# Order of the first stage, and of the last head pair, in an RWKV-7 and dilated-attention trunk

## What is computed

```python
h = rms_norm(x, mix_norm[0])
xx = jnp.pad(h, ((0, 0), (1, 0), (0, 0)))[:, :-1] - h      # token difference
x_mix = h[None] + xx[None] * mu[:, None, None, :]          # six mixes
rkv = jnp.einsum('cbsd,cde->cbse', x_mix[:3], w_rkv)       # receptance, key, value
w, a, g use x_mix[3], x_mix[4], x_mix[5] through low-rank products
...
outs, lses = per group: rms-normed q, k; banded softmax; o = probs v
weights = jax.nn.softmax(jnp.stack(lses), axis=0)
o = jnp.sum(weights[..., None] * jnp.stack(outs), axis=0) @ w_o
x = x + y; x = x + swiglu_ffn(rms_norm(x, ffn_norm[layer]), ...)
```

## Time and profile before

| | us |
|---|---|
| median of 3 runs | 1839.15 |
| profiled execution | 1842.12 |
| its span | 1840.3 |
| TensorE busy | 1799.3 |
| VectorE busy | 877.2 |
| ScalarE busy | 758.8 |

### The profile page before, as it was taken

How to read it: one execution, slowest core, us unless ns; L and a number is a source line. 1 busy time by engine, 2 the same in 40 slices (tenths; PEclk the granted TensorE clock), 3 DMA queues, 4 the chain that set the end, 5 groups by cost and what they waited for, 6 DMA issues and landing times.

```text
span 1840.3 us, 36149 instructions
## 1 busy us (share of the span) xinstructions
PE 1799.3 (98%) x15618; PEld 1371.4 (75%) x15618; DVE 877.2 (48%) x1513; ACT 758.8 (41%) x1292; POOL 196.8 (11%) x172
## 2 busy tenths in 40 slices
PE   8999999989999999999999999999999999999999
PEld 3746666656468888888888788788787788888887
DVE  6724444444264444433454654554555544444322
ACT  4434444432243223222456666666656542232211
POOL 0033333332100000000111111111010000000000
PEclk9999999989999999999999999999999999999999
DMA  3311222130123332323222222222222132323332
GB/s 113 118 64 51 75 68 67 63 120 29 36 80 103 94 101 92 103 92 103 93 80 92 81 65 86 81 71 79 81 75 86 51 99 93 103 92 96 100 102 92
DMA packets 57541, 155.00 MB, mean 84 GB/s; under 512 B 5591, under 2 KB 22535, under 8 KB 57384
## 3 DMA queue, kind: packets, MB, share of 16 engines
q1 hardware_dynamic: 57288, 152.63, 25.6%
q10 hardware_dynamic: 96, 0.07, 0.0%
HBM read 150.51 MB, written 11.61 MB: 88 GB/s over the span
## 4 chain that ended last, share of the span: by engine, by line
PE 69%; ACT 3%; DVE 1%; issue 1%; ACTq 0%
PE bank L548 67%; PE bank L551 2%; ACT f L1578 2%; DVE f L2094 0%; ACT f L1565 0%; ACT f L1591 0%; ACT r L1556 0%; ACT f L1552 0%; ACT f L1583 0%; ACT r L1268 0%; DVE r L1966 0%; DVE r L1682 0%; DVE f L2087 0%; ACT L1532 0%; ACT f L1279 0%
## 5 line engine op out<-in xcount | busy, mean ns | idle before, releaser
L548 PE MATMUL bank<-r 128*128 128x512 f32 x5424 | 1256.5, 391 | 1.9 <-DVE f L1999 0.7
L548 PEld LDWEIGHTS bank<-r 128*128 128x128 f32 x5424 | 1012.2, 188 | 225.1 <-issue 12.3
L548 PE MATMUL bank<-f 64*64 64x64 f32 (+5 forms) x9762 | 511.3, 257 | 30.5 <-issue 6.2
L548 PEld LDWEIGHTS bank<-f 64*64 64x64 f32 (+3 forms) x9762 | 311.2, 141 | 218.3 <-issue 126.4
L1682 DVE TENSOR_TENSOR r<-f,r 128x1024 fp32r<-128x1024 f32 x222 | 274.8, 1238 | 397.2 <-ACT r L1268 397.2
L1268 ACT ACTIVATE r<-f 128x1024 fp32r<-128x1024 f32 x222 | 232.5, 1048 | 147.7 <-PE bank L548 141.5
L2286 POOL TENSOR_TENSOR r<-f,r 128x512 fp32r<-128x512 f32 x48 | 62.1, 1295 | 845.0 <-ACT r L1556 845.0
L1535 ACT ACTIVATE r<-f 128x512 fp32r<-128x512 f32 x44 | 27.8, 632 | 215.6 <-DVE f L2005 215.6
L2035 DVE TENSOR_TENSOR f<-bank,f 128x512 f32<-128x512 f32 x72 | 56.2, 780 | 73.4 <-PE bank L548 70.1
L1532 ACT ACTIVATE f<-f 128x512 f32<-128x512 f32 x44 | 27.8, 632 | 110.5 <-DVE f L1995 110.5
L1565 ACT ACTIVATE f<-bank,f 128x512 f32<-128x512 f32 x48 | 32.9, 686 | 94.9 <-PE bank L548 94.9
(11 more groups left out here) (106 smaller groups left out, 911.9 us busy)
## 6 DMA issues: line engine op xcount, KB each, us to landing
f<-stream SPq DMA_DIRECT2D x245, 512.0 KB, 3.4
bias_copies<-bias_rows SPq DMA_DIRECT2D x6, 1536.0 KB
f<-xT SPq DMA_DIRECT2D x16, 256.0 KB, 4.5
f<-lora_out SPq DMA_DIRECT2D x16, 128.0 KB, 6.2
f<-bias_copies SPq DMA_DIRECT2D x16, 128.0 KB, 3.1
f<-bias_copies SPq DMA_DIRECT2D x32, 64.0 KB, 3.0
outT<-f SPq DMA_DIRECT2D x8, 256.0 KB, 4.4
f<-wo_last SPq DMA_DIRECT2D x2, 512.0 KB, 7.4
```

Of the source, the lines that this page charges most:

```text
L548: return nc.tensor.matmul(out, lhsT, rhs, start=start, stop=stop, skip_group_check=True)
```

## The change

In the first stage:
- ScalarE makes (1 - mu) h also for the value mixes (into `O_MIXV`) and the receptance mixes (into the temporaries), and VectorE adds mu h' in place. Value mixes no longer need the token differences.
- The token differences are made in pairs, ahead of each pair of decay and gate mixes, beside tiles 3 to 6.
- Both key tiles are multiplied chunk by chunk in turn, in banks 0 and 1; the value tile goes to bank 5.
- The value weights go to a place of their own (`O_VIN`), and the raw slots are counted accordingly.
- ScalarE's transfers of the bias rows come after the rounding of all receptance mixes and the split of panel `PAN_R + 1`.

In the last head pair: the three functions `last_pair` go. The general loop runs once more (`it` = 8) with the projection parts left out, and a table `EARLY` puts 14 chunks of output tiles 0 and 1 at four places. The other 50 chunks follow behind the combination of the last pair. Output tiles use two banks again, `ASIDE` goes, and weights before the feed-forward are split one panel later (`(n == 2)`).

```diff
-            if T_WO1 <= t < T_IN1:
-                return banks[(t - T_WO1) % 4]
...
-        ASIDE = {split_of(PAN_WO1 + 3): (O_XG + 4 * S, O_XG + 14 * S), split_of(PAN_WO1 + 4): (O_XG + 12 * S, O_QR)}
...
-                held = p - RAW - (RAW if p - RAW == PAN_WA else 0)
+                held = p - RAW - (RAW if p - RAW in (PAN_V, PAN_WA) else 0)
+                if p == PAN_V:
+                    sp.dma_start(f(O_VIN, 1024), stream[p]).then_inc(s["w_v"], 16)
+                    return
...
-                if T_WO1 + 2 <= t <= T_WO1 + 3:
-                    if part in (None, 0):
-                        att_read(pe, t - T_WO1, (t - T_WO1 - 2, 3), NHP - 1)
-                elif T_WO1 + 4 <= t <= T_IN1 + 1:
-                    pe.wait_ge(freed(t), t // 2 - 1)
-                elif t >= 2 and part in (None, 0) and not T_IN0 <= t <= T_IN0 + 2:
+                if t >= 2 and part in (None, 0) and not T_IN0 <= t <= T_IN0 + 2:
                     pe.wait_ge(freed(t), t // 2)
...
-            plain(PAN_K, O_MIXK, "mix_k")
-            plain(PAN_K + 1, O_MIXK, "mix_k")
+            for t in (PAN_K, PAN_K + 1):
+                raw_in(pe, t)
+            for c in range(KC):
+                pe.wait_ge(s["mix_k"], c + 1)
+                for t in (PAN_K, PAN_K + 1):
+                    last = mm(banks[t][:, :], raw(t, c), f(O_MIXK + c * S), c == 0, c == KC - 1)
+                    if c == KC - 1:
+                        last.then_inc(s["dense"], 1)
             pe.wait_ge(s["oh_in"], 32)
             for g in range(3):
                 mm(banks[2 + g][0:16, 0:384], f(O_REL + 16 * g, 16, 0, 33),
                    f(O_OH + 384 * g, 384, 0, 33)).then_inc(s["bias_ps"], 1)
-            plain(PAN_V, O_MIXV, "mix_v")
+            pe.wait_ge(s["w_v"], 16)
+            for c in range(KC):
+                pe.wait_ge(s["mix_v"], c + 1)
+                last = mm(banks[5][:, :], f(O_VIN + c * P, P), f(O_MIXV + c * S), c == 0, c == KC - 1)
+            last.then_inc(s["dense"], 1)
...
+            EARLY = {0: [(0, c) for c in range(5)], 1: [(1, 0), (1, 1), (1, 2)], 2: [(0, 5), (0, 6), (1, 3), (1, 4)],
+                     5: [(1, 5), (1, 6)]}
+            for it in range(NHP + 1):
                 a = it - 1
                 for i in range(9):
-                    t = T_QKV + 9 * it + i
-                    product(t, 8 * (PAN_QKV + 9 * it + i), lambda c: r(O_XG + c * S),
-                            lambda c: r(O_XG + (KC + c) * S), KC, "xg_lo" if it == i == 0 else None, KC)
+                    if it < NHP:
+                        t = T_QKV + 9 * it + i
+                        product(t, 8 * (PAN_QKV + 9 * it + i), lambda c: r(O_XG + c * S),
+                                lambda c: r(O_XG + (KC + c) * S), KC, "xg_lo" if it == i == 0 else None, KC)
                     if it == i == 0:
                         norm_sum(2)
-                    if i:
+                    if i and it < NHP:
                         projection_aux(it, i - 1)
                     if a < 0:
                         continue
@@ -1194,52 +1185,12 @@
                         flip_probs(a, 1, i - 3)
                     if i == 7:
                         lse_difference(a)
-            def last_pair(a):
-                def heads(m, *chunks):
-                    for c in chunks:
+                    for m, c in EARLY.get(i, []) if it == NHP else []:
                         projected_heads(m, c)
-                heads(0, 0)
-                projection_aux(a, 8)
-                logits(a, 0)
-                heads(0, 1, 2)
-                logits(a, 1)
-                heads(0, 3, 4)
-                logits(a, 2)
-                heads(0, 5)
-                heads(1, 0)
-                logits(a, 3)
-                heads(1, 1, 2)
-                flip_probs(a, 0, 0)
-                heads(1, 3, 4)
-                flip_probs(a, 1, 0)
-                heads(1, 5)
-                heads(2, 0)
-                flip_probs(a, 0, 1)
-                attend(a, 0)
-                heads(2, 1, 2)
-                flip_probs(a, 1, 1)
-                heads(2, 3)
-                flip_probs(a, 0, 2)
-                attend(a, 1)
-                flip_probs(a, 1, 2)
-                lse_difference(a)
-                flip_probs(a, 0, 3)
-                attend(a, 2)
-                flip_probs(a, 1, 3)
-                heads(2, 4, 5)
-                attend(a, 3)
-                heads(3, 0, 1, 2, 3)
-                for m in range(3):
-                    heads(m, 6)
-                heads(3, 4, 5, 6)
-                for m in range(4):
-                    heads(m, KC - 1)
-            last_pair(NHP - 1)
-            for m in range(4, KC):
+            att_read(pe, 7, None, NHP - 1)
+            for m in range(2):
+                projected_heads(m, KC - 1)
+            for m in range(2, KC):
...
-                    elif q in ASIDE:
-                        full(act, T_WO1 - 1)
...
+            def key_part(k):
                 act.wait_ge(s["h"], k + 1)
                 if k == 0:
-                    act.wait_ge(s["one_mu"], 1)
-                A(f(O_XX + k * S), hk(k), ACT.Identity, scale=f(O_SM + 48 + k, 1)).then_inc(s["h_part"], 1)
+                    act.wait_ge(s["one_mu"], 3)
+                A(f(O_XX + k * S), hk(k), ACT.Identity, scale=f(O_SM + 48 + k, 1)).then_inc(s["key_part"], 1)
+            def value_part(k):
+                A(f(O_MIXV + k * S), hk(k), ACT.Identity, scale=f(O_SM + 56 + k, 1)).then_inc(s["value_part"], 1)
+            def receptance_part(k):
+                if k >= N_TMP:
+                    act.wait_ge(s["mix_lo"], k - N_TMP + 1)
+                A(f(O_TMP + k % N_TMP * S), hk(k), ACT.Identity, scale=f(O_SM + 64 + k, 1)).then_inc(s["mix_part"], 1)
+            for k in range(KC):
+                key_part(k)
+                if k % 2:
+                    value_part(k // 2)
+            for k in range(KC // 2, KC):
+                value_part(k)
+            for k in range(N_TMP):
+                receptance_part(k)
...
+            for i in range(KC):
+                round_mixed(i)
+                if i == 1:
+                    split_high(PAN_R)
+                if 1 <= i < KC - N_TMP + 1:
+                    receptance_part(i + N_TMP - 1)
+                if i == 5:
+                    take(PAN_V, O_VIN)
+            split_high(PAN_R + 1)
             for g in range(3):
                 act.wait_ge(s["bias_sb"], g + 1)
                 rows = bias_rows[g * 16 * 384:(g + 1) * 16 * 384].rearrange("(h u) -> h u", h=16)
                 act.dma_start(rows, f(O_E + g * 384, 384, 0, 16)).then_inc(s["bias_dma"], 16)
-            for i in range(3):
-                round_mixed(i)
-            split_high(PAN_R)
-            round_mixed(3)
-            take(PAN_V, O_VIN)
-            for i in range(4, KC):
-                round_mixed(i)
-            split_high(PAN_R + 1)
...
-                        split_high(p_of(t0 + m) + LEAD + (n == 2))
+                        split_high(p_of(t0 + m) + LEAD)
...
-            def last_pair(a):
-                projection_aux(a, 8)
-                split_high(PAN_WO1 + 3)
-                exps(a, 0, 0)
-                exps(a, 1, 0)
-                split_high(PAN_WO1 + 4)
-                keep_flipped(a, 0, 0)
-                exps(a, 0, 1)
-                keep_flipped(a, 1, 0)
-                exps(a, 1, 1)
-                keep_flipped(a, 0, 1)
-                combine(a - 1)
-                nc.scalar.preload_act_table_set("sigmoid_and_others")
-                keep_flipped(a, 1, 1)
-                keep_flipped(a, 0, 2)
-                keep_flipped(a, 1, 2)
-                keep_near(a)
-                sigmoid_weights(a)
-                keep_flipped(a, 0, 3)
-                keep_flipped(a, 1, 3)
-                combine(a)
-            last_pair(NHP - 1)
+                        act.wait_ge(s["attended"], 4 * a + 2)
+                        if a:
+                            act.wait_ge(s["att_lo"], a)
+                        free(A(f(O_OA), banks[6][:, :], ACT.Copy), 6)
+            combine(NHP - 1)
...
+            for n, mu in enumerate(("mu1", "mu2", "mu0")):
+                TS(f(O_SM + 48 + n * KC, KC), f(O_PV + VECS.index(mu) * KC, KC), -1.0, 1.0, ALU.mult, ALU.add)\
+                    .then_inc(s["one_mu"], 1)
...
-            for k in range(KC + 1):
-                if k < KC:
-                    dve.wait_ge(s["mix_k"], k + 1)
-                    TT(f(O_XX + k * S), hk(k, 1), hk(k), ALU.subtract).then_inc(s["xx"], 1)
-                if k:
-                    dve.wait_ge(s["xx"], k)
-                    STT(f(O_MIXV + (k - 1) * S), f(O_XX + (k - 1) * S), vec("mu2", k - 1), hk(k - 1),
-                        ALU.mult, ALU.add).then_inc(s["mix_v"], 1)
+            for k in range(KC):
+                dve.wait_ge(s["value_part"], k + 1)
+                STT(f(O_MIXV + k * S), hk(k, 1), vec("mu2", k), f(O_MIXV + k * S), ALU.mult, ALU.add)\
```

(54 more changed lines are left out.)

65 lines of the change are left out of this document (25 added, 40 removed).

## The result

| | us |
|---|---|
| after, median of 4 runs | 1849.7 (1846.06 to 1851.85) |
| before, 4 runs beside them | 1838.22 (1836.2 to 1839.68) |
| ratio, 95% interval | 1.0046 (1.0031 to 1.0062) |
| profiled execution after | 1850.99 |
| its span | 1849.2 |

What follows compares the result with a forecast made beforehand. The prediction took TensorE, busy 98% of the span, as the bound. First stage -1.5, last pair's order +9.6 and clock +1.7 gave +9.8 us: 1842.12 to 1851.9 profiled, median 3.0 lower, 1849.0, range 1844.6 to 1854.9.

Steps and rivals of the forecast that it cites:

- First stage: From the key tiles to the second receptance tile, which was to start at 48.85 instead of 50.34: 1.5 us gained.
- both tiles end at 33.1: Key tiles in the first stage: start 17.68, plus 13.7 us of matmuls, plus 1.7 us for low clock.
- The step on the transfers: First stage: the moved bias transfers hold ScalarE's next split until 49.8, needed at 54.3, so beside TensorE.
- The low clock at the start: Key tiles, 17.68 to 24 us: granted clock 0.73, formerly hidden by slack behind the mixes, now costs 1.7 us.
- Last pair, order: Last head pair: the general loop instead of the written-out order loses 9.6 us at full clock through TensorE's gaps.
- Last pair, clock: Last head pair: half clock behind the two long gaps costs 1.7 us together, bounds nothing and about 5.
- the first row: First clock window before the change, 17.68 to 24 us, 0.73 of full clock: taken as 1.7 us per long gap.
- Sum: Whole kernel: -1.5 + 9.6 + 1.7 = +9.8 us, median forecast 1849.0 us, chance 0.66.
- Rival 1: Last pair: half clock stays through its sparse second half and merges with the next gap, 3 to 4 us more; 0.13.
- Rival 2: First stage gains nothing because ScalarE, with 11.1 us of work in 11, falls behind VectorE: 1850.5 us; 0.10.
- Rival 3: Last pair: ScalarE's table load costs more than its record, so the last rounding waits 1.1 us: 1850.1 us; 0.05.
- Rival 4: Last pair: the general order costs nothing, both gaps (4.2 and 3.7 us) vanish, not slower: 1837.2 us; 0.06.

Runs made afterwards that it cites:

- experiment 6: Kernel 1 with ScalarE's three bias transfers back right behind the bias copies: 1841.67 us, ratio 0.9996 to the kernel before.
- experiment 5: Kernel 1 with key tile 0 multiplied wholly before key tile 1, as before: 1842.71 us, ratio 1.0005 to the kernel before.
- experiment 4: The changed kernel with four unread float32 matmuls in each of the last pair's two long gaps: 1848.11 us, ratio 1.0048 to the kernel before.
- experiment 2: The kernel before with only the last-pair part of the change (general loop): 1852.12 us, ratio 1.0066 to the kernel before.
- experiments 9 and 10: The kernel before with seven unread matmuls in the scan, 1841.3 us; kernel 1 with the same seven, 1839.5 us (the changed kernel with them, 1852.94 us).
- kernel 1: The kernel before with only the first-stage part of the change, hand-written last pair kept: 1841.63 us, ratio 0.9997 to the kernel before.

## Why the prediction was right

- **The bound.** Right: both kernels have 1799 us of TensorE's work, and the difference is idle and half-clock time.
- **First stage.** Forecast -1.5, measured -1.84. Counted from the first key matmul (17.68 in the forecast, 17.26 in after), "both tiles end at 33.1" is 15.4, and the last key copy starts at 15.7; the first low part is at 18.6 in the forecast and at 18.8 in after. The 0.34 us lie behind it: the second panel's low split was forecast to end at 31.1, and the first of the two passes from 46.71 ends at 30.6. The step on the transfers, "now hold ScalarE's next split until 49.8", was wrong: beside the roundings they hid. At their old place (experiment 6) they cost 0.8 to 1.0 us, not the 1.3 that the forecast put on them. The low clock at the start, forecast at 1.7 us, took 1.7: (1 - 0.76) x 6.32 = 1.5 in the window, which misses the first 0.42 us of the run at half clock. Taking turns is worth 1.0 us even so (experiment 5).
- **Last pair, order.** Forecast 9.6, measured 9.5 at full clock (experiment 4). The long gaps are where they were put: 4.2 forecast and 4.18 measured, 3.7 and 3.68, and 0.7 and 0.78 for the one ahead of the last products. Of the small ones, 0.9 ahead of tile 2 came out at 0.36 (experiment 4), 1.1 ahead of the pair at 0.78, and the 0.25 at 1428.3 isn't seen. That the sum fits to 0.1 us is partly luck.
- **Last pair, clock.** This is the term that was mis-sized: 1.7 forecast, 2.8 measured. The working took 1.7 us for each gap, from the first row, and let the idle time behind it take back 0.85 and 0.7; by its own terms that makes 1.85, not 1.7. Behind the second gap the low clock took (1 - 0.59) x 3.82 = 1.6 and 0.1 more by 1456, as forecast. Behind the first it lasted longer than at the start: 5.3 us at 0.50 and one more at 0.68, 3.0 us. Of these 4.7 us idle time took back 1.9. So what was mis-sized is the length of the low clock behind the first gap.
- **Outside.** -1.2 us between the first stage and the last pair were not forecast, nor were the 0.4 us at the start. The clock near 112 us, low before and full after, holds 0.8 of the 1.2.
- **Sum.** Together 9.8 forecast and 8.9 measured between the spans, 8.5 on the ratio. That 1849.0 met the median of 1849.7 so closely is luck: the last pair's clock was 1.1 us short, the first stage and the part outside made up for it and more, and medians of four executions scatter by more than a microsecond. The four of before lie at 1838.2, the 81 others at 1842.2.
- **Rival 1** (the half clock merges; 1852.5): not so, though it was the nearest. The low clock behind the first gap lasted 2.5 us longer than that at the start, but it ended before 1441, ahead of the second gap, and the pair's 2.8 us are below the rival's 1.7 + 3.
- **Rival 2** (nothing gained in the first stage): not so; 1.84 us in the trace, 1.8 between the medians of experiments 9 and 10, and ScalarE waits for VectorE 1.2 us there, not the other way round in steady work.
- **Rival 3** (the table load costs more than its record): not seen. The rounding at 1448.68 starts 0.02 us after VectorE's step ended. The load ends 0.25 us ahead of it, so up to that much beyond its record would not show. The Trainium skill (ScalarE: Activation LUTs, "What ACT_TABLE_LOAD costs") adds about 1.38 us to a load; this case's trace doesn't agree with that figure, which would have put the rounding at 1449.8.
- **Rival 4** (not slower): excluded by experiment 2. The pairs 0 to 6 run this order at no cost because projections lie between its steps; with 16 chunks left there is nothing to issue.

What stays open: why the mean clock of 16 to 26 us is 0.66 in some executions and 0.83 in others with the same code ahead of it, why after is 0.7 us faster between 190 and 233 us, and what in the middle of the last pair, if not ScalarE's order, would shorten the first gap.

## What to carry to other kernels

A general loop costs nothing as long as it has other work between its dependent steps; its last round, which has none, wants an order of its own, and its price can be stepped through from the rows of a round that is covered. Where a change makes gaps of several us on TensorE, look in the trace for the longest stretch of low clock that follows such a gap, and take the forecast's upper bound from it. A gain of 1 or 2 us is read from the stretch of the trace in which it arises, on a common starting point, when totals spread over 10 us.

## What the runs showed of the hardware

The spread of the kernel before, 1835.6 to 1847.3 us, follows the mean granted clock of the execution. At 0.999 it took 1835.6 to 1838.7, at 0.993 and 0.994 it took 1841.8 to 1847.3; over all runs 0.001 less clock goes with 1.4 us more. In the traces the largest stretch of it is at the end of the scan: TensorE is busy 7.86 of 12 us from 380 to 392, and then runs at 0.57 of full clock from 396 to 408 in before, and from 392 to 404 in after. In the profiled executions of kernel 1 and of experiments 4 and 5 the mean from 380 to 425 us is 1.00, with the same code. So it is not a fixed cost, and the half clock, 1.2 instead of 2.4 GHz, follows a sparse stretch in some executions and not in others. The Trainium skill (TensorE: Matmul & The Clock Gate, "What's actually happening") has throttled as the default, which activity releases; the trace agrees, and shows beside it that the same sparse stretch can go either way. Unread matmuls keep the clock up where TensorE is idle anyway (1.1 to 2.1 us at the start, by how long the low clock would have lasted, and 2.8 us in the last pair). In the scan, where TensorE is 60 to 65% busy and others wait for it, they cost 2.9 us, and give back 3.9 where the low clock would have come.
